# Where the next head's key and query tiles stand in PE's order in prompt attention

## The reference, cut to what matters

```python
q, k, v, u, g_att, g_s5 = split(rms_norm(x) @ w_in)
p   = softmax(q1 @ k1.T / 8, causal) - lam * softmax(q2 @ k2.T / 8, causal)   # 8 heads, two halves of 64
att = rms_norm(p @ v, per head) * (1 - lam_init)
x   = x + (sigmoid(g_att) * att @ w_proj_att + sigmoid(g_s5) * s5 @ w_proj_s5) @ w_out
x   = x + PEER(rms_norm(x))      # 8 product-key heads, 16 gathered expert rows for each
```

## Time and profile before

| what | value |
|---|---|
| median of 3 runs | 4465.69 us (4462.35 to 4467.46) |
| the profiled execution | 4462.64 us, of which the span is 4460.9 us |
| mean granted clock of PE | 0.908 of full |
| busy share | PE 75%, PEld 43%, DVE 68%, ACT 34%, POOL 30% |
| DMA | 1416.84 MB, mean 318 GB/s |
| attention, chunk 0 / 1 / 2 | about 533 to 658, 1059 to 1346, 1876 to 2240 us |

### The profile page before, as it was taken

One profiled execution on the slowest core, in us unless ns is written; L12 is line 12 of the kernel. 1 busy time (PEld: TensorE's weight loads), 2 busy tenths in 40 slices (PEclk: granted clock), 3 DMA queues, 4 the chain that ended last, 5 costly groups with the idle time before them and its releaser, 6 DMA issues. The chain is left out here.

```text
span 4460.9 us, 43476 instructions
## 1 busy us (share of the span) xinstructions
PE 3361.5 (75%) x13280; PEld 1915.9 (43%) x13280; DVE 3039.5 (68%) x6500; ACT 1502.3 (34%) x3882; POOL 1323.9 (30%) x1168
## 2 busy tenths in 40 slices
PE   7857979787768869877668758877777777777776
PEld 4646666544434444344456634432222222222221
DVE  6473021788888878877776758886676676666664
ACT  2121140333553324254443323223333333333332
POOL 0100000233223333322233323344444444444442
PEclk9878989998879889988888969999999999999999
DMA  3117425998778999966699979899999999999997
GB/s 130 18 3 105 146 86 179 369 394 340 261 271 347 362 383 392 409 211 228 221 364 402 405 266 417 327 412 419 419 418 416 412 413 413 412 412 400 411 407 304
DMA packets 284909, 1416.84 MB, mean 318 GB/s; under 512 B 47459, under 2 KB 88899, under 8 KB 147587
## 3 DMA queue, kind: packets, MB, share of 16 engines
q0 software_dynamic: 159344, 1129.94, 63.5%
q1 hardware_dynamic: 124946, 283.98, 18.7%
q10 hardware_dynamic: 384, 0.13, 0.0%
HBM read 1370.00 MB, written 42.11 MB: 317 GB/s over the span
## 5 line engine op out<-in xcount | busy, mean ns | idle before, releaser
L911 POOL DMA_INDIRECT arena<-in_uv,arena x1056 | 1248.5, 1182 | 2312.9 <-DVE arena L1024 1417.6
L1014 DVE CUSTOM_DVE_ANT_0 arena<-arena 128x1024 f32<-128x1024 f32 x1056 | 1288.9, 1222 | 510.4 <-DMA arena<-in_uv,arena 481.9
L1132 PE MATMUL ps<-arena 128*128 128x512 f32 (+1 forms) x2288 | 1086.6, 620 | 404.3 <-ACT arena L1101 404.3
L656 PE MATMUL ps<-arena 128*128 128x256 f32 (+2 forms) x3456 | 1109.4, 481 | 146.6 <-DMA arena<-in_w_stat 68.3
L656 PEld LDWEIGHTS ps<-arena 128*128 128x128 f32 x3456 | 682.7, 201 | 536.9 <-issue 354.1
L1132 PEld LDWEIGHTS ps<-arena 128*128 128x128 f32 (+1 forms) x2288 | 413.4, 190 | 1076.9 <-ACT arena L1101 629.1
L1024 DVE SCALAR_TENSOR_TENSOR arena<-arena 128x1024 f32<-128x1024 f32 x484 | 618.9, 1279 | 18.7 <-ACT arena L1091 18.7
L1082 ACT ACTIVATE arena<-arena 128x2 f32<-128x2 f32 x528 | 107.2, 203 | 1533.1 <-DVE arena L1014 1514.8
L1091 ACT ACTIVATE arena<-arena 128x1 f32<-128x1 f32 x1056 | 253.4, 287 | 17.7 <-ACT arena L1082 0.5
L1082 ACT ACT_TABLE_LOAD x156 | 200.1, 1283 | 46.0 <-PEq L1260 28.9
L1101 ACT ACTIVATE arena<-ident,arena 128x128 f32<-128x128 f32 x540 | 187.2, 394 | 8.8
(11 more groups left out here) (251 smaller groups left out, 3294.7 us busy)
## 6 DMA issues: line engine op xcount, KB each, us to landing
arena<-in_w_stat SPq DMA_DIRECT2D x216, 512.0 KB, 7.8
arena<-in_cache_k SPq DMA_DIRECT2D x64, 512.0 KB, 10.7
arena<-in_cache_v SPq DMA_DIRECT2D x64, 512.0 KB, 11.5
arena<-in_w_mov SPq DMA_DIRECT2D x14, 2048.0 KB, 14.5
arena<-in_uv,arena POOLq DMA_INDIRECT x1056, 13.1
arena<-in_x SPq DMA_DIRECT2D x16, 512.0 KB, 9.2
arena<-scr_s POOLq DMA_DIRECT2D x64, 128.0 KB, 12.9
scr_s<-arena SPq DMA_DIRECT2D x16, 384.0 KB, 15.2
```

The costliest lines, as they stand in the source:

```text
L656: last = nc.tensor.matmul(ps[:, bank, 0:w], wbuf[m % NWB][:, kc * P:(kc + 1) * P], moving[:, kc, :], start=(kc == 0), stop=(kc == KC - 1))
L911: pool.indirect_dma_start(ring[s % RING], None, dr["uv"], bass.IndirectOffsetOnAxis(ap=idx[:, g % 4, j:j + 1], axis=0)).then_inc(row_in[s ...
L1014: nc.vector.tensor_tensor_reduce(ring[s % RING][:, 0:D], ring[s % RING][:, 0:D], h2r[:, b % 2, :], 1.0, 0.0, ALU.mult, ALU.add, act_in[:, ...
L1132: last = nc.tensor.matmul(ps[0:m, 4 * (b % 2) + c, :], diag[:, n % 4, 0:m], ring[s % RING][:, D + 512 * c:D + 512 * (c + 1)], start=start, ...
```

## The change

It moves `k_tile(h + 1)` from behind T0 to ahead of PE's wait for the probabilities in unit nf-2, and `q_tile(h + 1)` from behind T1 to ahead of the wait in unit nf-1. In chunks 1 and 2 these are the second and third units of a head, in chunk 0 the first and second. `q_in` on ACT moves to unit nf-1, `k_in` on DVE to the end of unit nf-2; in chunk 0 that is still unit 0, and there `normalised(h - 1)` now comes ahead of it. No instruction is added or taken away.

```diff
                             if i + 1 < nf:
                                 scores(h, i + 1)
+                            if more and i == nf - 2:
+                                k_tile(h + 1)
+                            if more and i == nf - 1:
+                                q_tile(h + 1)
                             pe.wait_ge(p_ready, u + 1)
...
                             last.then_inc(t_ready, 1)
-                            if more and i == 0:
-                                k_tile(h + 1)
-                            if i == 1:
-                                if h:
-                                    pe.wait_ge(o_free, u)
-                                    turn_outputs(h - 1)
-                                if more:
-                                    q_tile(h + 1)
+                            if i == 1 and h:
+                                pe.wait_ge(o_free, u)
+                                turn_outputs(h - 1)
                             pe.wait_ge(t_free, u + 1)
...
-                            if more and i == 1:
+                            if more and i == nf - 1:
                                 q_in(h + 1)
                             peer_act(act, share(c, "att", h * nf + i + 1, H * nf))
...
                             peer_dve(dve, share(c, "att", h * nf + i + 1, H * nf))
-                            if i == 0:
-                                if more:
-                                    k_in(h + 1)
-                                if h:
-                                    normalised(h - 1)
+                            if i == 0 and h:
+                                normalised(h - 1)
+                            if i == nf - 2 and more:
+                                k_in(h + 1)
```

## The result

The changed kernel takes 4525.02 us (median of 4 runs, 4519.98 to 4530.13) against 4464.02 us before (4 runs): a ratio of 1.0137, interval 1.0123 to 1.0151, so 61 us slower. I had 4538, between 4492 and 4572.

A forecast was written before the change was run, and what follows sets the result against it. No engine is full; turns of PE, ACT and DVE in a head set the attention stages. Delays of 26, 25 and 21 us sum to 72, giving 4538 us beside the median, with 0.8 between 4492 and 4572.

The forecast's parts named there:

- The deciding step: All chunks: the query tile waits for `k_in`, DVE's last work before `probabilities`, so it cannot fill PE's wait for them.
- what I said the profile would show: PE's query tile waits for `k_in`, some 3 us in chunk 0, 2 to 8 elsewhere; probabilities waits nearly gone except last heads.
- The terms: Delays of the three attention stages, shifts plus slower clock: 26, 25 and 21 us, together 72.
- the clock: PE's clock falls behind longer waits, 2.3 us for less than half of the query tiles: 6, 5 and 9 us by stage.
- The shifts at full clock: Later steps in each head from the query tile's wait, clock aside: 20, 20 and 12 us in chunks 0, 1, 2.
- 2.8 us later in each head: Chunk 1: the query tile delays T2 and O2, 2.8 us at full clock for each of seven heads.
- the 1.7 us a head: Chunk 2: mean delay for each of seven heads, from 0.4 us with one pair in unit 1 and 2 with two.
- My rival with every tile slow: All stages: the clock falls for every tile, 2.3 us on all 20, giving 4564 and up to 4580 us; chance 0.16.
- the sum of a head: Chunk 0, a head T0 to T0: 4.5, tile 3.6, 2.1, 4.5 and key tile 3.6, 18.3 us against 14.7.
- The key tile at nothing in chunks 1 and 2: Moving it from behind T0 to behind `scores(h, 2)` costs nothing on average, both places lying under DVE's pair of unit 0.
- That the tiles fill the waits: Rival: both tiles run inside PE's 89.2 us of probabilities waits if `k_in` is done well before; 4442 us; chance 0.05.
- The drain: Chunk 0: about 1.38 us added per table load would lengthen the chain 1.4 us, the sum 8 us over six heads.

The follow-up runs named there:

- e3: The changed kernel with DVE copying the key tile at once, ahead of its pair and the normalising; 4441.06 us, ratio 0.9946 to the kernel before.
- e4: The kernel before with only the query tile (and `q_in`) moved ahead of the last unit's wait, key tile and key copy in old places; 4438.96 us, ratio 0.9945.
- e5: The changed kernel with the query tile writing its own PSUM bank in chunk 0, key copy still late; 4490.65 us, ratio 1.0065 to the kernel before.
- e7: The changed kernel with 24 idle transposes in chunk 0 ahead of the query tile's wait for the key copy; 4508.43 us, ratio 1.0102 to the kernel before.
- e1: The changed order in chunk 0 only, chunks 1 and 2 as in the kernel before; 4492.24 us, ratio 1.0071 to the kernel before.
- e6: The changed kernel with the key tile back behind the first transposes, key copy still late; 4499.98 us, ratio 1.0077 to the kernel before.
- control: The kernel before, unchanged, timed against itself; 4463.95 us, ratio 0.9999.

## Why the prediction was right, and where it was off

*The deciding step held.* I had said that `k_in`, behind DVE's pair and just ahead of `probabilities`, makes the query tile start when the wait is all but over. The waits for L1581 (75.6 us in 22), e3 and e4 (waits of 1.9 and 4.0 us, loss gone) and e5 (another bank, wait gone) show it from three sides. The range held the time, and 61 us against 72 is near; that it is so near is in part luck, as the terms show. Of what I said the profile would show, the wait in chunk 0 was 2.9 us (some 3), in the others 0.7 to 10.2 (2 to 8), and the waits for the probabilities fell to 6 of 26; but a head of chunk 0 took 20.4 us, not 18.

*The terms.* By stage I had 26, 25 and 21; the profile has 30.5, 20.3 and 14.1. The split was off more than the sum. At full clock I had 52 (20, 20 and 12), and 34 is left when the 31 of slower tiles are taken off the 65 (14.6, 8.2 and 10.7; by PE's waits alone 13.6, 2.9 and 13.6); for the clock I had 20 (6, 5 and 9). So two terms were mis-sized, and the errors cancelled. The clock was put too low in chunks 0 and 1: I let it fall for less than half of the query tiles, and in this profile 18 of 21 ran slow (6 of 7, 7 of 7 and 5 of 7), the key tiles of chunk 0 with them. In chunk 2 it was put too high: 9 us, where PE's work as a whole took no longer than before. The shifts at full clock were put too high in chunks 0 and 1, most of all in chunk 1, where I had T2 and O2 come 2.8 us later in each head and let no later step give any of it back; PE's waits there for `exps` and `output_in` shrank by 5.1 and 3.7 us. In chunk 2 the 1.7 us a head isn't the mean of its two cases, 0.4 and 2, and nothing in the rows gives it. My rival with every tile slow was nearly right on the number of tiles, and its time, 4564, was too high, because the terms at full clock were too large and because its 46 us for the clock were 31: several tiles had run slow before the change. In chunk 0 the sum of a head was 18.3 us, and e7 shows 17.1 at full clock: the tile started 4.06 us behind T0 and not 4.5, T1 to `k_by_token` took 1.8 and not 2.1, and from there over the key tile to T0 7.6 and not 8.1.

*The key tile at nothing in chunks 1 and 2.* Right as far as told: 0 to 4 us either way in the table of four, no more than two profiles of one code differ.

*The rivals.* That the tiles fill the waits was wrong for this change, and nearer the truth than I had thought for the idea: with the key copy on time they fill some 30 of the 89 us (e3, e4), and e3's 4441 is near the 4442 that this rival had given for a copy done well before the wait. 0.05 was the chance of the change as written, not of the idea. Filler work in the wait kept the clock (e7: tiles in 3.72 us instead of 5.41). By the rule of the Trainium skill (TensorE: Matmul & The Clock Gate, "Part 1: The HAM clock gate"), an idle PE is put to half rate; e7 agrees. The length of the wait alone doesn't tell here: behind 1.24 us a tile of chunk 1 ran slow (7.12 us instead of 5.33), and behind 2.94 us one of e1 ran fast. The drain that the Trainium skill (ScalarE: Activation LUTs, "What ACT_TABLE_LOAD costs") adds to a table load does not show in these rows: the Sqrt follows the load within 0.01 us, the load follows the exponentials' last instruction within 0.02, and the chain came out shorter than my sum, not longer.

*What stays open.* What sets which of the two clock patterns a run of chunk 0 falls into wasn't tried, nor was a run made that holds the clock in chunks 1 and 2.

## What to carry to other kernels

Before a step is moved into a wait, ask what the step itself waits for and where that stands in the other engine's list: here the copy that the filler waited for, to have its PSUM bank free, was done by the very engine, and just ahead of the very instruction, that the wait was for. See that this step stays early when the filler moves, and try each of several moves alone: the query tile's move by itself won 0.35 to 0.55%, with the late key copy it lost 0.8% (e6), and with the key tile moved too 1.4%.

## What the runs showed that I had not expected

One code ran at two clocks behind the same wait of 2.9 us: the heads of chunk 0 took 20.4 us each in one profile and, from the fourth head on, 17.1 in another, with the query tile at 5.41 or 3.72 us. And 24 transposes that compute nothing, 2.78 us a head, made the changed kernel 17 us faster. The medians of the old kernel and its control lie 1.4 us apart, while single executions of it spread over 4449 to 4476.
